# A three-part change to the expert stage of a one-core transformer kernel: a new deal of token slots over partitions, one 24 KB-row transfer per expert into four slots, and the residual parked in DRAM

## The reference

```
scores = sigmoid(h @ w_router)                 # 512 tokens x 64 experts
top_e  = 8 experts of each token (group-limited)
w      = 2.5 * scores[top_e] / sum(scores[top_e])
for each expert e:                             # only its own tokens
    gate, up = split(h[tok] @ w_gu[e])         # w_gu[e]: 1024 x 512
    acc[tok] += w * ((silu(gate) * up) @ w_down[e])   # w_down[e]: 256 x 1024
out = acc + shared_expert(h)
x   = x + gain * rms_norm(out)                 # x is the residual, 512 x 1024
```

## Time and profile before

| | |
|---|---|
| Time, median of 3 runs | 2174.39 us (2172.56 to 2180.85) |
| The profiled execution's own time | 2177.97 us |
| Its span | 2176.2 us, so 1.8 us lie around it |
| Granted TensorE clock, mean | 0.988 |
| PE busy | 2071.2 us, 95% |
| DVE, ACT, POOL busy | 1226.0, 963.1 and 245.0 us |
| Expert stage: first and last gate-up product | 570.7 to 1304.3 us |
| DMA, mean over the span | 180 GB/s |

### The profile page before, as it was taken

One profiled execution on the slowest core, in us unless ns is written; L12 is line 12 of the kernel. 1 busy time (PEld: TensorE's weight loads), 2 busy tenths in 40 slices (PEclk: granted clock), 3 DMA queues, 4 the chain that ended last, 5 costly groups with the idle time before them and its releaser, 6 DMA issues.

```text
span 2176.2 us, 32844 instructions
## 1 busy us (share of the span) xinstructions
PE 2071.2 (95%) x12130; PEld 1677.2 (77%) x12131; DVE 1226.0 (56%) x2035; ACT 963.1 (44%) x1349; POOL 245.0 (11%) x217
## 2 busy tenths in 40 slices
PE   7999979999999899999989998999999999999998
PEld 3788977789767567676666666998988898899898
DVE  4859577455756556766656657456653344423433
ACT  4347375223456456665556654234332224312322
POOL 0004022000122122222223220000000000000000
PEclk9999999999999999999999999999999999999999
DMA  9921111263788779999989975211112223222221
GB/s 355 294 101 60 54 45 61 95 246 147 291 296 311 259 246 331 342 350 334 346 277 326 355 264 191 97 59 59 53 65 97 97 74 111 97 97 89 88 96 59
DMA packets 76667, 392.52 MB, mean 180 GB/s; under 512 B 16321, under 2 KB 32833, under 8 KB 46049
## 3 DMA queue, kind: packets, MB, share of 16 engines
q1 hardware_dynamic: 57506, 357.33, 44.0%
q0 software_dynamic: 19008, 33.22, 6.2%
HBM read 384.03 MB, written 42.48 MB: 196 GB/s over the span
## 4 chain that ended last, share of the span: by engine, by line
PE 57%; DMA 9%; DVE 4%; issue 2%; ACT 2%; POOLq 0%; DVEq 0%; SPq 0%; ACTq 0%; POOL 0%
PE bank L3326 16%; DMA ffn_sums<-moe_work 6%; PE bank L2265 6%; PE bank L2243 4%; PE bank L2247 3%; PE bank L2246 3%; PE bank L3009 3%; PE bank L3010 3%; PE bank L3011 3%; PE bank L2994 2%; PE bank L2996 2%; PE bank L2995 2%; PE bank L2231 2%; DMA moe_work<-h_rows,moe_work 2%; DVE moe_gu_rest L2024 1%
## 5 line engine op out<-in xcount | busy, mean ns | idle before, releaser
L2611 DVE TENSOR_TENSOR b_w_rest<-ring,b_w_high 128x2048 fp32r<-128x2048 f32 x63 | 144.4, 2292 | 181.6 <-ACT b_w_high L2606 181.2
L2265 PE MATMUL bank<-moe_work 128*128 128x512 f32 x512 | 237.7, 605 | 4.1 <-issue 4.0
L2243 PE MATMUL bank<-moe_gu_high,moe_x_high 128*128 128x512 f32 x512 | 210.3, 411 | 15.8 <-issue 9.5
L2024 DVE TENSOR_TENSOR moe_gu_rest<-moe_work,moe_gu_high 128x2048 fp32r<-128x2048 f32 x64 | 143.8, 2288 | 122.1 <-ACT moe_gu_high L1773 122.1
L2024 DVE TENSOR_TENSOR moe_gu_rest<-ring,moe_gu_high 128x2048 fp32r<-128x2048 f32 x64 | 143.8, 2289 | 114.3 <-ACT moe_gu_high L1773 114.3
L2247 PE MATMUL bank<-moe_gu_high,moe_x_rest 128*128 128x512 f32 x512 | 204.0, 398 | 0.0
L2246 PE MATMUL bank<-moe_gu_rest,moe_x_high 128*128 128x512 f32 x512 | 203.7, 398 | 0.0
L2606 ACT ACTIVATE b_w_high<-ring 128x2048 fp32r<-128x2048 f32 x63 | 120.5, 1912 | 177.3 <-PE bank L3326 126.8
L3010 PE MATMUL bank<-b_w_rest,b_h_high 128*128 128x256 f32 x608 | 172.9, 284 | 0.0
L2265 PEld LDWEIGHTS bank<-moe_work 128*128 128x128 f32 x512 | 92.2, 190 | 95.2 <-issue 94.8
L3009 PE MATMUL bank<-b_w_high,b_h_high 128*128 128x256 f32 x544 | 157.1, 289 | 2.2 <-DVE b_h_rest L2641 1.1
(11 more groups left out here) (509 smaller groups left out, 4957.2 us busy)
## 6 DMA issues: line engine op xcount, KB each, us to landing
ring<-in_stream_dram SPq DMA_DIRECT2D x105, 1024.0 KB, 4.9
moe_work<-in_experts_dram SPq DMA_DIRECT2D x32, 2048.0 KB, 14.7
moe_work<-in_experts_dram SPq DMA_DIRECT2D x64, 1024.0 KB, 9.5
ring<-in_experts_dram SPq DMA_DIRECT2D x32, 2048.0 KB, 15.9
X<-in_stream_dram SPq DMA_DIRECT2D x16, 512.0 KB, 8.4
mixer_work<-in_stream_dram SPq DMA_DIRECT2D x16, 512.0 KB, 6.8
X<-in_x_dram SPq DMA_DIRECT2D x8, 512.0 KB, 8.4
ffn_sums<-mixer_work SPq DMA_DIRECT2D x8, 512.0 KB, 5.5
```

The lines of the kernel that those rows point to most:

```text
L2024: v.tensor_tensor(WL[o % 4][h], guslot[o % 4][:, HALF * h:HALF * (h + 1)], WH[o % 2][h], ALU.subtract).then_inc(s["w_rest"], 1)
L2243: first = mm(banks[2][:, :], xh[:, k, :], wh[h][:, c], start=(k == 0), stop=False)
L2265: product = mm(banks[bank + j][:, :], HDT[o % 2][:, k, :], w[:, k, 512 * j:512 * (j + 1)], start=(k == 0), stop=(k == 1))
L2611: nc.vector.tensor_tensor(WL[u % FEED], raw(u), high_at(u), ALU.subtract).then_inc(s["w_rest"], 1)
```

## The change

**The slots' deal.** `DEALT` decides which partition holds which rank. Before, rank 16a+b sits at partition 8b+a, so the first 64 ranks sit at the partitions whose number modulo 8 is 0 to 3. After, rank 64b+16d+8a+c sits at partition 64a+32b+4c+d: ranks 0 to 15 go to partitions 0, 4, ... 28 and 64, 68, ... 92, the next 16 to the partitions behind these, and the first 64 ranks fill partitions 0 to 31 and 64 to 95. The same token rows are moved by the same two indirect DMAs.

**The weights.** Each of four slots takes gate-up and down of an expert by one transfer of 3 MB with 24 KB rows. It waits for `dn_done` alone.

**The residual.** For the room that this takes, `X` goes to DRAM (`residual_rows`) at the end of the mixer, the high parts of even experts' weights (`WH[0]`) move into the place of `X`, and `X` comes back at the end of the stage. `SHARED_DOWN` moves into slot 1 and is loaded a step earlier.

```diff
@@ mixer, SP
             for t in range(NT):
+                sp.wait_ge(s["mixed"], t + 1)
+                sp.dma_start(dram["x"][t * P:(t + 1) * P, :], X[:, t, :]).then_inc(s["x_stored"], 16)
                 sp.wait_ge(s["h2_ready"], t + 1)
                 sp.dma_start(dram["xn"][t * P:(t + 1) * P, :], H2[:, t, :]).then_inc(s["h2_stored"], 16)
             sp.wait_ge(s["h2_stored"], 16 * NT)
+            sp.wait_ge(s["x_stored"], 16 * NT)
@@ moe, places
-    GU_AT = [AT_WORK, AT_WORK + GU, 0, GU]
-    guslot = [part(0, GU), part(GU, GU), mem["ring"][:, 0:GU], mem["ring"][:, GU:2 * GU]]
-    dnslot = [part(2 * GU, DN), part(2 * GU + DN, DN)]
+    SLOT = GU + DN
+    SLOT_AT = [AT_WORK, AT_WORK + SLOT, 0, SLOT]
+    slot = [part(0, SLOT), part(SLOT, SLOT), mem["ring"][:, 0:SLOT], mem["ring"][:, SLOT:2 * SLOT]]
+    guslot, dnslot = [a[:, 0:GU] for a in slot], [a[:, GU:SLOT] for a in slot]
-    WH_AT = [[4 * UNIT, 5 * UNIT], [AT_WORK + F_AT + 2 * D, AT_ADAROW + D]]
+    WH_AT = [[AT_X, AT_X + HALF], [AT_WORK + F_AT + 2 * D, AT_ADAROW + D]]
-    SHARED_DOWN = mem["ring"][:, 5 * UNIT:6 * UNIT]
+    SHARED_DOWN = part(2 * GU, UNIT)
@@ moe, SP
-            for e in (3, 2):
+            for e in (0, 1, 3, 2):
                 if e == 2:
                     sp.wait_ge(s["sh_full"], 4)
-                sp.dma_start(guslot[e], experts[e, :, 0:GU]).then_inc(s_gu[e], 16)
+                sp.dma_start(slot[e], experts[e, :, :]).then_inc(s_w[e], 16)
             with sp.Fori(1, NE // 4) as i:
                 for u in range(4):
-                    sp.wait_ge(s["gu_begun"], 4 * i + (u - 2))
-                    sp.dma_start(guslot[u], experts[index(i, u), :, 0:GU].rearrange("a p c -> (a p) c")).then_inc(
-                        s_gu[u], 16)
                     sp.wait_ge(s["dn_done"], 4 * i + (u - 3))
-                    sp.dma_start(dnslot[u % 2], experts[index(i, u - 2), :, GU:].rearrange("a p c -> (a p) c")).then_inc(
-                        s_dn[u % 2], 16)
-            for e in (NE - 2, NE - 1):
-                sp.wait_ge(s["dn_done"], e - 1)
-                sp.dma_start(dnslot[e % 2], experts[e, :, GU:]).then_inc(s_dn[e % 2], 16)
+                    sp.dma_start(slot[u], experts[index(i, u), :, :].rearrange("a p c -> (a p) c")).then_inc(s_w[u], 16)
+            sp.wait_ge(s["dn_done"], NE - 2)
+            sp.dma_start(SHARED_DOWN, stream[LOADU[2]]).then_inc(s["shared_down_in"], 16)
             sp.wait_ge(s["gu_begun"], NE)
-            sp.dma_start(SHARED_DOWN, stream[LOADU[2]]).then_inc(s["shared_down_in"], 16)
+            for t in range(NT):
+                sp.dma_start(X[:, t, :], dram["x"][t * P:(t + 1) * P, :]).then_inc(s_xback[t], 16)
@@ moe, ACT, w_high
-                act.wait_ge(s_gu[o % 4], 16 * (o // 4 + 1) + 16 * i)
+                act.wait_ge(s_w[o % 4], 16 * (o // 4 + 1) + 16 * i)
@@ moe, DVE
-            link(v.tensor_copy(DEALT.rearrange("p (b a) -> p b a", b=16), slots.rearrange("p (a b) -> p b a", b=16)))
+            for a in range(2):
+                for b in range(2):
+                    of_half = slots[:, 64 * b:64 * b + 64].rearrange("p (d a c) -> p a c d", d=4, a=2)
+                    last = v.tensor_copy(grid(DEALT[:, 64 * a + 32 * b:64 * a + 32 * b + 32], 8), of_half[:, a, :, :])
+            link(last)
...
+                dve.wait_ge(s_xback[t], 16)
                 v.scalar_tensor_tensor(out=X[:, t, :], in0=FR[:, t, :], scalar=FS2[:, t:t + 1], in1=X[:, t, :],
@@ moe, PE, down_ready
-                pe.wait_ge(s_dn[o % 2], 16 * (o // 2 + 1) + 32 * i)
+                pe.wait_ge(s_w[o % 4], 16 * (o // 4 + 1) + 16 * i)
```

More of the change, by code:

```diff
@@ L178, in program @@
             "sums": [nc.dram_tensor(f"ffn_sums{k}", [TOK, D], F32) for k in range(2)],
+            "x": nc.dram_tensor("residual_rows", [TOK, D], F32),
         }
@@ L325, in mixer @@
              "h2_mean", "h2_root", "h2_ready", "ht_full", "ht_act", "ht_dve", "wr_in", "rows_ready", "zero_ready",
-             "zero_stored", "h2_stored", "dve_order")
+             "zero_stored", "h2_stored", "x_stored", "dve_order")
     s = {n: sem(n) for n in names}
@@ L1436, in moe @@
     GU, DN, HALF = 4096, 2048, 2048
-    GU_AT = [AT_WORK, AT_WORK + GU, 0, GU]
-    guslot = [part(0, GU), part(GU, GU), mem["ring"][:, 0:GU], mem["ring"][:, GU:2 * GU]]
-    dnslot = [part(2 * GU, DN), part(2 * GU + DN, DN)]
-    at = [2 * GU + 2 * DN]
+    SLOT = GU + DN
+    SLOT_AT = [AT_WORK, AT_WORK + SLOT, 0, SLOT]
+    slot = [part(0, SLOT), part(SLOT, SLOT), mem["ring"][:, 0:SLOT], mem["ring"][:, SLOT:2 * SLOT]]
+    guslot, dnslot = [a[:, 0:GU] for a in slot], [a[:, GU:SLOT] for a in slot]
+    at = [2 * SLOT]
     def take(width):
@@ L1465, in moe @@
     XGL = [grid(exact(f"x_rest{k}", AT_WORK + spare + D * k, D), KD) for k in range(2)]
-    WH_AT = [[4 * UNIT, 5 * UNIT], [AT_WORK + F_AT + 2 * D, AT_ADAROW + D]]
+    WH_AT = [[AT_X, AT_X + HALF], [AT_WORK + F_AT + 2 * D, AT_ADAROW + D]]
     WH = [[exact(f"gu_high{k}{h}", WH_AT[k][h], HALF) for h in range(2)] for k in range(2)]
-    WL = [[exact(f"gu_rest{k}{h}", GU_AT[k] + HALF * h, HALF) for h in range(2)] for k in range(4)]
+    WL = [[exact(f"gu_rest{k}{h}", SLOT_AT[k] + HALF * h, HALF) for h in range(2)] for k in range(4)]
     OVER = FF[:, 0:2 * D]
@@ L1504, in moe @@
     IDXX, WCX = [EXR[:, 512 + k:513 + k].bitcast(I32) for k in range(2)], [EXR[:, 514 + k:515 + k] for k in range(2)]
-    JUNK2, ROWC = part(2 * GU + DN, D), part(2 * GU + D, D)
+    JUNK2, ROWC = part(2 * GU + DN, D), part(2 * GU + DN + D, D)
     LAST = NE // 4 - 1
@@ L1528, in moe @@
     s_back = [sem(f"sums_back{t}") for t in range(NT)]
-    s_gu = [sem(f"gate_up_arrived{k}") for k in range(4)]
-    s_dn = [sem(f"down_arrived{k}") for k in range(2)]
+    s_xback = [sem(f"residual_back{t}") for t in range(NT)]
+    s_w = [sem(f"weights_arrived{k}") for k in range(4)]
     s_gath = [sem(f"gathered{k}") for k in range(4)]
@@ L2260, in down_ready @@
                     after(pe, "out_act", i, o - 1, 2, 2)
-                pe.wait_ge(s_dn[o % 2], 16 * (o // 2 + 1) + 32 * i)
+                pe.wait_ge(s_w[o % 4], 16 * (o // 4 + 1) + 16 * i)
             def down_part(i, o, j, k, bank=4):
-                w = dnslot[o % 2].rearrange("p (k c) -> p k c", k=2)
+                w = dnslot[o % 4].rearrange("p (k c) -> p k c", k=2)
                 product = mm(banks[bank + j][:, :], HDT[o % 2][:, k, :], w[:, k, 512 * j:512 * (j + 1)],
@@ L2317, in further_down @@
                 pe.wait_ge(s["x_he"], n + 1)
-                pe.wait_ge(s_dn[u % 2], 16 * (u // 2 + 1) + 32 * i)
-                w = dnslot[u % 2].rearrange("p (k c) -> p k c", k=2)
+                pe.wait_ge(s_w[u % 4], 16 * (u // 4 + 1) + 16 * i)
+                w = dnslot[u % 4].rearrange("p (k c) -> p k c", k=2)
                 for j in range(2):
```

## The result

| | before | after |
|---|---|---|
| Median | 2175.82 us | 2183.79 us |
| Runs (lowest to highest) | 20 (2171.14 to 2184.33) | 20 (2174.67 to 2190.75) |
| Ratio, with its 95% interval | | 1.003 (1.0017 to 1.0044) |
| Span of the profiled execution | 2176.2 us | 2179.8 us |

The forecast of 2165.5 us was wrong by 18 us, of which 1.4 us are the kernel before, whose median is 2175.82 us here against 2174.39 us. The measured time lies at the upper end of the range. The interval of the ratio lies wholly above 1: a small loss, where a small gain was forecast.

What follows compares the result with a forecast made beforehand. PE, busy 95% of the span, was taken to bound the kernel, leaving 12.8 us of expert-stage stall to win. Terms -12.0 + 0.5 + 0.7 + 0.3 + 0.5 + 1.0 = -9.0 us gave 2165.5 us, range 2158 to 2184.

Steps and rivals of the forecast that it cites:

- How long is it?: Expert stage, 3 MB weight load: lands after 11.3 us, hidden behind the preceding expert's products; +0.5 us for single late ones.
- The limit of 12.3 us: Expert stage: the 3 MB load must land within 12.3 us of issue, 11.7 us lead plus 0.6 us slack.
- the ceiling of 11.8 us: Upper bound on the load's landing, from gate-up and down issued 0.6 us apart and landed after 11.8 us, from 785 us.
- A load that is late by x delays PE by about x/2 an expert: Expert stage: two experts lie between a slot's release and its use, so lateness costs (x / 2) x 55 ordinary experts.
- The deal, -12.0: Two stalled expert stretches: spreading the first 64 ranks over 16 engines instead of eight wins 12.0 us.
- the bound of -12.8: Upper bound of the slots' gain: all 12.8 us of stall in two expert stretches go if the queue hides the last tenth.
- 24 KB rows beside indirect rows, +0.7: Around the three experts of more than 128 tokens, indirect rows wait longer for weight rows: +0.7 us, bounds 0 and 3.
- The copies of the deal, +0.3: DVE's chain to the routing tables: four copies replace one of 0.27 us, +0.3 us, bounds 0 and 0.8.
- Residual and its stores, 0: End of the mixer: residual stores ahead of the `h` stores hide behind the norm, 0 us, at most +0.5, 2.9 if unhidden.
- the tail, +1.0: End of the expert stage: the last scatter meets the four transfers bringing X back, +1.0 us, bounds 0 to 3.
- Code fetch, +0.5: Program code fetched over the same engines may be held up by longer weight rows: +0.5 us, range 0 to 2.
- the load comes too late: Expert stage rival, chance 0.16: weights land late and slow the kernel, about 2198 us at 13.5 us landing, 2184 at 13.0.

Runs made afterwards that it cites:

- deal alone: The kernel before with only the new `DEALT` placement of ranks, weights and residual untouched: 2158.75 us, ratio 0.9904 to the kernel before.
- gate-up early again: Changed kernel with the expert load cut in two, gate-up issued on its old wait (begin of a gate-up product): 2162.03 us, ratio 0.9917 to the kernel before.
- two transfers at the same moment: Changed kernel with gate-up and down issued together as separate transfers, each with its own semaphore: 2165.84 us, ratio 0.9923 to the kernel before.
- five sixths of the bytes: Changed kernel loading 20 KB of each 24 KB row from the fifth expert on, output not the reference's: 2163.27 us, ratio 0.9912 to the kernel before.
- run with one wait: Changed kernel with gate-up and down issued together as two transfers on one semaphore, every wait being for both: 2186.77 us, ratio 1.0024 to the kernel before.

## Why the prediction was wrong, by its own steps

Where the time went is seen when the expert stage of three profiled executions is cut at the starts of gate-up products on the timeline of PE (first expert to last in us):

```
experts         0-10   11-15  16-33  34-44  45-47  48-60  61-62   sum
before         121.4    86.4  187.1  122.6   49.2  137.5   24.5  728.7
deal alone     118.1    86.2  186.9  113.0   49.6  133.5   21.9  709.2
after          117.4    90.8  190.2  117.1   52.1  138.9   25.3  731.8
```

**The step that failed: "How long is it? ... I take it at 11.3, hidden behind the gate-up, `turn` and `down` of the expert before, and charge +0.5."** The load lands after a median of 12.8 us, and the two lower rows say what that costs: 731.8 - 709.2 = 22.6 us. The limit of 12.3 us was right, and so was the time of a quiet load. Wrong was the ceiling of 11.8 us, read from 785 us on, where the stage has just begun anew. For that stretch it was right: in the changed kernel the loads from 785 to 840 us have a median of 11.4 us. Later it is not. With the engines full (a share of 0.99 in the changed kernel), a load issued every 10.3 us that takes longer than that would meet its predecessor in the queue (argued, as above), and where experts are larger, as from 965 us on, the gathers and scatters beside it are larger, too. The row that should have been the bound stood next to it: 18.8 to 20.8 us in the crowded stretch, put aside because "others" were queued ahead. Part of that queue was the indirect rows, and they stayed.

**"A load that is late by x delays PE by about x/2 an expert"** had the loop wrong, which spans three experts and not two. For loads that are all late alike the loop of the chain gives x / 3. But these landings scatter, from 11.1 to 13.5 us for experts 34 to 44, and the latest of each three counts, so the loss lies above x / 3 of the median. The loads of experts 34 to 44 have a median of 13.0 us and those of experts 48 to 60 one of 13.1 us (the 13.8 us above are of the loads behind 1205 us, for experts 57 on). By the medians x / 3 gives 2.6 and 3.5 us against 4.1 and 5.4 measured, and x / 2 gives 3.9 and 5.2, which is nearer, but not for the reason given. With each load's own landing put into the loop (a gate-up product begins 10.27 us behind the last one, or 18.51 us plus the landing behind the one three experts earlier, whichever is later) it comes to 3.3 and 4.9 us, 8.2 of the 9.5. More than half of the 22.6 us lies in ordinary experts: 3.3 + 4.1 + 5.4 = 12.8. Another 4.6 + 2.5 + 3.4 = 10.5 lies around the three experts of more than 128 tokens and in the last two, -0.7 in the first eleven. What waits for what in these places was not followed to its end. With gate-up early again they take 89.1, 49.6 and 21.5 us, so the last two losses are gone with it. But the last is not one of landing: with two transfers at the same moment, and with five sixths of the bytes, experts 61 and 62 still take 25.6 and 25.0 us. The first (90.8 us) may be nothing. Over all profiled executions that piece lies anywhere from 84.9 to 90.8 us, and it is 86.7 us in the run with one wait, which is as slow as the changed kernel.

**The deal, -12.0,** had the right mechanism and too small a size: the deal alone gave 1% of 2176, or 19.6 us of the stage. In the two stretches that were named the stall went wholly (9.6 of 9.6 us, and with the neighbours of the second 4.0), which is the bound of -12.8 and not the 0.93 x 11.15 = 10.37. The windows say why: a share of 1.01 can be reached here, and I had taken the mean of 0.93 to leave a tenth of stall. Missed were 2.6 us at experts 61 and 62. The chain of the kernel before had a gather there whose time was not looked at, since I counted scatters only: 

```profile
1264.87 16.09 DMA moe_work<-h_rows,moe_work
```

The 3.3 us in the first eleven experts may be nothing: over all profiled executions of the study this piece lies anywhere from 115.8 to 124.7 us.

**24 KB rows beside indirect rows, +0.7:** the prediction wanted ACT's wait for scatters under 15 us. It is 32.3 us in the changed kernel, and 8.8 in the deal alone and 4.2 in the run with one wait and shorter rows. So these rows do make scatters late, but by the run with one wait they cost no time beyond what the late load costs anyhow. **The copies of the deal, +0.3:** four in 0.47 us for one in 0.27, right. **Residual and its stores, 0, and the tail, +1.0:** the tail costs nothing (877.0 against 876.9 us), the whole round trip 0 to 7 us by its run; right within that. **Code fetch, +0.5:** not separated.

**The rivals.** What happened was the one called "the load comes too late", held at 0.16. Its price list (landing 13.0 gives 2184) meets the measured time, but by luck: it has 12.0 us for a deal that gave 19.6, 19.3 us for lateness that cost 22.6, and 2.5 us of other terms of which no run shows more than a part, and these errors largely cancel. Its point of decision, 12.65 us, was right in kind and the landing was over it. The chances leaned on the pair at 11.8 us as evidence against it, a row from the wrong stretch. They were also added up wrongly: by the shares given for each case "same" is 0.25 + 0.15 + 0.02 = 0.42 and not 0.40.

## What to carry to other kernels

A transfer's landing time is a property of the queue as well as of its bytes. If a change shortens the lead, take the landing from the most crowded stretch in which it will run, and find the loop that the transfer closes: the time of as many experts as it spans, less the rest of the loop, is the limit for the transfer. An even lateness is divided by the number of experts that the loop spans; where landings scatter, the latest of each round counts. When one transfer replaces two, ask who waits for its first part, since now he waits for its last byte. And where indirect rows and weights share the engines, count the rows on the fullest engine: this one edit of a table of constants was worth 1%.

## What was not expected

- PE and the 16 DMA engines can both be full at once for 113 us (PE busy 113.00 of 113.00, DMA share 1.01, 361 GB/s) with no stall. A deal of the same bytes that is uneven ends at 0.93 and 339 GB/s, with just eight packets under way for 0.08 of the time.
- Taking half a megabyte from each load of 3 MB shortened its landing by 2.7 us, twice what the bytes take in a quiet queue.
- Issuing a 2 MB load 6 us later, under the new deal, cost nothing and brought its median landing from at least 13.6 us to 9.5.
